# One phase for the second layer's norm, token mix, 28 projection products and key norm, with x and its squares handed over in SBUF

## What is computed

```python
def _rms(x, g):
    y = x * lax.rsqrt(jnp.mean(x * x, axis=-1, keepdims=True) + RMS_EPS)
    return y * g

x  = x + conv_ffn(...)                     # layer 0 ends; its last step is the down projection
h  = _rms(x, norm_mix[1])
xx = 0.5 * (previous token + next token of h) - h      # zero beyond the ends of each group
xr, xw, xk, xv, xa, xg = (h + xx * mu[i] for i in range(6))
r, k, v = xr @ w_r, xk @ w_k, xv @ w_v                 # 1024 x 1024 each
w = tanh(xw @ w1); a = xa @ a1; g = sigmoid(xg @ g1)   # narrow: 128, 128 and 160 columns
kk = k * k_k, divided by its length within each head of 64 channels
```

## Time and profile before

| | us |
|---|---|
| median of 3 runs | 5436.38 |
| lowest and highest of them | 5423.24, 5439.86 |
| the profiled execution, its own time | 5390.18 |
| its span, first to last instruction | 5388.3 |
| its mean granted TensorE clock | 0.887 of full speed |

### The profile page before, as it was taken

How to read it: one execution, slowest core, us unless ns; L and a number is a source line. 1 busy time by engine, 2 the same in 40 slices (tenths; PEclk the granted TensorE clock), 3 DMA queues, 4 the chain that set the end, 5 groups by cost and what they waited for, 6 DMA issues and landing times. The chain is left out here.

```text
span 5388.3 us, 97136 instructions
## 1 busy us (share of the span) xinstructions
PE 4514.7 (84%) x41700; PEld 3690.8 (68%) x41700; DVE 2352.2 (44%) x4075; ACT 1312.4 (24%) x2687; POOL 1311.0 (24%) x915
## 2 busy tenths in 40 slices
PE   2999798999999938876567777777767899999997
PEld 1789667888888827765355555555555588888886
DVE  3011262442425251123577777777773224234341
ACT  1111372111111122222233333333332221111110
POOL 2111133111111101110344444444441131111110
PEclk8999899999999979997587877877788699999998
DMA  3112334113131222211311111111102231221314
GB/s 125 58 59 72 92 97 118 44 48 106 36 117 39 91 69 70 70 59 60 102 41 46 46 41 47 51 39 43 51 31 76 57 105 39 88 65 60 96 35 164
DMA packets 393901, 371.41 MB, mean 69 GB/s; under 512 B 61408, under 2 KB 358752, under 8 KB 392336
## 3 DMA queue, kind: packets, MB, share of 16 engines
q1 hardware_dynamic: 377616, 336.52, 20.4%
q10 hardware_dynamic: 15872, 28.84, 1.4%
HBM read 263.06 MB, written 102.24 MB: 68 GB/s over the span
## 5 line engine op out<-in xcount | busy, mean ns | idle before, releaser
L417 POOL TENSOR_TENSOR f_wlow<-f_raw,f_whigh 128x1024 fp32r<-128x1024 f32 (+1 forms) x152 | 360.2, 2370 | 1678.8 <-ACT f_whigh L477 1678.8
L462 PE MATMUL f_ps<-fx_hh,f_whigh 128*128 128x512 f32 (+1 forms) x2112 | 529.0, 359 | 0.0
L462 PE MATMUL f_ps<-fx_hl,f_whigh 128*128 128x512 f32 (+1 forms) x2112 | 528.0, 359 | 0.0
L462 PE MATMUL f_ps<-fx_hh,f_wlow 128*128 128x512 f32 (+1 forms) x2112 | 527.6, 358 | 0.0
L523 DVE TENSOR_TENSOR f_xo<-f_ps,f_xo 128x512 f32<-128x512 f32 (+1 forms) x192 | 103.7, 596 | 698.9 <-PE f_ps L462 661.0
L477 ACT ACTIVATE f_whigh<-f_raw 128x1024 fp32r<-128x1024 f32 (+1 forms) x152 | 156.7, 1031 | 987.3 <-PE f_ps L462 960.2
L462 PEld LDWEIGHTS f_ps<-fx_hl,f_whigh 128*128 128x128 f32 x2112 | 351.9, 188 | 62.4
L462 PEld LDWEIGHTS f_ps<-fx_hh,f_wlow 128*128 128x128 f32 x2112 | 351.8, 188 | 62.4
L462 PEld LDWEIGHTS f_ps<-fx_hh,f_whigh 128*128 128x128 f32 x2112 | 352.1, 189 | 61.8
L1537 PE MATMUL sc_inv_ps<-sc_tf,sc_bl 64*64 64x64 f32 x6400 | 318.8, 249 | 78.7 <-DVE sc_tf L1878 74.1
L462 PE MATMUL f_ps<-mo_oh,f_whigh 128*128 128x512 f32 (+1 forms) x1440 | 361.3, 359 | 25.4 <-POOL f_wlow L417 25.4
(11 more groups left out here) (318 smaller groups left out, 8720.3 us busy)
## 6 DMA issues: line engine op xcount, KB each, us to landing
f_xo<-xres SPq DMA_DIRECT2D x64, 640.0 KB, 4.0
xres<-f_xo SPq DMA_DIRECT2D x64, 640.0 KB, 2.9
f_raw<-in_ffn_w_gate SPq DMA_DIRECT2D x44, 512.0 KB
f_raw<-in_ffn_w_up SPq DMA_DIRECT2D x44, 512.0 KB
sc_rk<-rkvl SPq DMA_DIRECT2D x80, 256.0 KB, 3.2
f_raw<-in_ffn_w_down SPq DMA_DIRECT2D x32, 448.0 KB
qkv_raw<-in_na_w_qkv SPq DMA_DIRECT2D x24, 512.0 KB, 5.5
qkn<-qkv_qk SPq DMA_DIRECT2D x16, 640.0 KB, 3.6
```

The costliest lines, as they stand in the source:

```text
L417: nc.gpsimd.tensor_tensor(wlow[:, m % 2, 0:kt], raw[:, 0:kt], whigh[:, m % 2, 0:kt].bitcast(F32), ALU.subtract).then_inc(cut_lo, 1)
L462: last = nc.tensor.matmul(ps[:, m % 2, n, 0:count], w[:, m % 2, k], x[:, k, t0:t0 + count], start=(k == 0 and w is whigh and x is xh), sto ...
```

## The change

1. `feed_forward` gets two more outputs. In the last 8 down jobs of layer 0, DVE writes its sum into a kept SBUF tensor `x` and no longer into `xo` (the store to `xres` stays); ACT squares each tile and POOL adds the squares up in `total`.
2. `rms_norm`, `mix_differences`, the six `mixed_product` phases and `unit_keys` go. A new `rwkv_inputs` is one phase. It sums `total` over channels on TensorE, takes root and reciprocal of 128x10 numbers, spreads them to 128x1280 in PSUM, and DVE multiplies `x` by that in place ("normalise"). POOL forms the neighbour sums `near`. The norm's gain and the mix weights are folded into two scales by channel, so a mixed tile is ACT's scaled copy of `x` ("own") plus DVE's `near` times a scale ("blend").
3. The 28 jobs run in the order r, v, w, a, g, k. ACT mixes the tiles of the next kind when its list reaches the last job of the kind before. One buffer `raw` of weights takes the place of two.
4. In the k jobs, ACT squares a finished tile of k, TensorE sums within heads between steps of the next job and spreads the inverted roots, and DVE scales the tile where it lies; SP stores it to `kks`.

```diff
@@ feed_forward, SP, POOL, ACT, DVE
+                    src = x_out[:, i] if x_out is not None and residual[q] >= last_down else xo[:, q % 2]
+                    sp.dma_start(xres[:, i], src).then_inc(stored[q % 2], 16)
...
+                def add_square(i):
+                    pool.wait_ge(last_squared, i + 1)
+                    if i >= 2:
+                        pool.wait_ge(last_totalled, i - 1)
+                    nc.gpsimd.tensor_tensor(total_out[:], total_out[:], square, ALU.add).then_inc(last_totalled, 1)
...
+                    if m >= last_down and x_out is not None:
+                        act.wait_ge(evicted, m + 1)
+                        if i >= 2:
+                            act.wait_ge(last_totalled, i - 1)
+                        nc.scalar.activation(square if i else total_out[:], x_out[:, i], ACT.Square).then_inc(last_squared, 1)
...
+                            old = dst
+                            if m >= last_down and x_out is not None:
+                                dst = x_out[:, i, t0:t0 + count]
+                            last = nc.vector.tensor_tensor(dst, src, old, ALU.add)
@@ new rwkv_inputs: SP
+                sp.dma_start(ones[:], consts["ones"][:, 0:2]).then_inc(small_in, 16)
+                sp.dma_start(ident[:], consts["ident"]).then_inc(small_in, 16)
+                sp.dma_start(block64[:], consts["block64"]).then_inc(small_in, 16)
+                load_weights(0)
...
+                load_weights(1)
+                for m in range(NJ):
+                    if m + 2 < NJ:
+                        load_weights(m + 2)
+                    store(m)
+                    if m >= K0 + 1:
+                        store_key(m - K0 - 1)
@@ POOL
+                low(0)
+                low(1)
+                for k in range(KT):
+                    pool.wait_ge(normed, k + 1)
+                    for a, b in ((1, T_PROMPT - 1), (T_PROMPT + 1, T - 1)):
+                        nc.gpsimd.tensor_tensor(near[:, k, a:b], x[:, k, a - 1:b - 1], x[:, k, a + 1:b + 1], ALU.add)
+                    nc.gpsimd.tensor_copy(near[:, k, 0:T_PROMPT + 1:T_PROMPT], x[:, k, 1:T_PROMPT + 2:T_PROMPT])
+                    nc.gpsimd.tensor_copy(near[:, k, T_PROMPT - 1:T:T_SAMPLE], x[:, k, T_PROMPT - 2:T - 1:T_SAMPLE]).then_inc(near_done, 1)
+                for m in range(2, NJ):
...
+                    low(m)
@@ TensorE
+                for m, (n, i) in enumerate(jobs):
+                    pe.wait_ge(cut_lo, m + 1)
...
+                    for k in range(KT):
+                        if i == 0:
+                            pe.wait_ge(mix_lo, order.index(n) * KT + k + 1)
...
+                        if m >= K0 + 1:
+                            if k == 2:
+                                key_sums(m - K0 - 1)
+                            if k in (4, 5, 6):
+                                key_roots(m - K0 - 1, k - 4)
@@ ACT
+                def own(j):
+                    c, k = divmod(j, KT)
+                    if j >= 3:
+                        act.wait_ge(mix_lo, j - 2)
...
+                    nc.scalar.activation(slot(j), x[:, k], ACT.Copy, scale=own_scale[:, r, k:k + 1]).then_inc(own_done, 1)
...
+                def mix(c):
+                    own(c * KT)
+                    own(c * KT + 1)
+                    for k in range(KT):
+                        if k + 2 < KT:
+                            own(c * KT + k + 2)
+                        high(c * KT + k)
...
+                mix(0)
+                for m, (n, i) in enumerate(jobs):
+                    if m == last_of[n] and n != "k":
+                        mix(order.index(n) + 1)
+                    leave(m)
+                    if m + 2 < NJ:
+                        cut(m + 2)
+                    if n == "k":
+                        key_root(i)
@@ DVE
+                def normalise(k):
+                    nc.vector.tensor_tensor(x[:, k, 0:1024], flat(1), x[:, k, 0:1024], ALU.mult)
+                    nc.vector.tensor_tensor(x[:, k, 1024:T], ps[:, 1, 2, 0:256], x[:, k, 1024:T], ALU.mult).then_inc(normed, 1)
...
+                def mix(c):
+                    for k in range(KT):
+                        blend(c * KT + k)
+                        if k:
+                            low(c * KT + k - 1)
+                        if c == 0 and k + 2 < KT:
+                            normalise(k + 2)
+                    low(c * KT + KT - 1)
```

More of the change, by code:

```diff
@@ L1048, in mixed_product, with rwkv_inputs @@
-def mixed_product(nc, name, h, xx, mu, sources, func, out, out_tile, xh, xl):
-    n, load_tile, zero_first = sources
-    with Phase(nc, name) as ph:
-        raw = ph.sb("raw", [P, 2, KT, P])
-        wh = ph.sb("wh", [P, 2, KT, P], F32R)
-        wl = ph.sb("wl", [P, 2, KT, P], F32R)
+def rwkv_inputs(nc, x, total, gain, mu, w_r, w_k, w_v, w1, a1, g1, k_k, rkvl, kks, consts):
+    rest = g1.shape[1] - P
+    order = "rvwagk"
+    views = {n: w.rearrange("(k p) n -> p k n", p=P) for n, w in zip("rwkvag", (w_r, w1, w_k, w_v, a1, g1))}
+    mu_row = {n: i for i, n in enumerate("rwkvag")}
+    tiles = {"r": KT, "v": KT, "w": 1, "a": 1, "g": 2, "k": KT}
+    out_tile = {"r": 0, "k": KT, "v": 2 * KT, "w": 3 * KT, "a": 3 * KT + 1, "g": 3 * KT + 2}
+    func = {"r": ACT.Copy, "k": ACT.Copy, "v": ACT.Copy, "w": ACT.Tanh, "a": ACT.Copy, "g": ACT.Sigmoid}
+    jobs = [(n, i) for n in order for i in range(tiles[n])]
+    NJ = len(jobs)
+    last_of = {n: max(m for m, job in enumerate(jobs) if job[0] == n) for n in order}
+    K0 = jobs.index(("k", 0))
+    width = lambda m: rest if jobs[m] == ("g", 1) else P
+    halves = (slice(0, HD), slice(HD, P))
+    with Phase(nc, "ri") as ph:
+        xh = ph.sb("xh", [P, KT, T], F32R)
+        xl = ph.sb("xl", [P, KT, T], F32R)
+        near = ph.sb("near", [P, KT, T])
@@ L1063, in mixed_product @@
+        flat = lambda b: ps[:, b, 0:2].rearrange("p g n -> p (g n)")
+        slot = lambda j: total[:] if j % 3 == 2 else mixed[:, j % 3]
         with nc.Block() as block:
@@ L1065, in _, with load_weights @@
             def _(sp):
[L1066 to L1077 removed]
+                def load_weights(m):
+                    n, i = jobs[m]
+                    if m:
+                        sp.wait_ge(cut_lo, m)
+                    if jobs[m] == ("g", 1):
+                        sp.wait_ge(cleared, 1)
+                    sp.dma_start(raw[:, :, 0:width(m)], views[n][:, :, i * P:i * P + width(m)]).then_inc(w_in, 16)
@@ new lines, in _ @@
+                dve.wait_ge(summed, 1)
+                nc.vector.tensor_scalar(rc[:], sums[:, 0:NB], 1.0 / D, RMS_EPS, ALU.mult, ALU.add).then_inc(averaged, 1)
+                dve.wait_ge(rooted, 1)
+                nc.vector.reciprocal(rc[:], rc[:]).then_inc(inverted, 1)
+                dve.wait_ge(gain_in, 128)
+                for n in range(6):
+                    last = nc.vector.tensor_tensor(mus[:, n], mus[:, n], g[:], ALU.mult)
+                last.then_inc(mu_gain, 1)
+                dve.wait_ge(mu_gain, 1)
@@ new lines, in blend, with low @@
+                def blend(j):
+                    c, k = divmod(j, KT)
+                    r = mu_row[order[c]]
+                    dve.wait_ge(own_done, j + 1)
+                    if c == 0:
+                        dve.wait_ge(near_done, k + 1)
+                    nc.vector.scalar_tensor_tensor(slot(j), near[:, k], near_scale[:, r, k:k + 1], slot(j), ALU.mult, ALU.add).then_inc(mix_done, 1)
+                def low(j):
+                    k = j % KT
+                    dve.wait_ge(mix_hi, j + 1)
+                    nc.vector.tensor_tensor(xl[:, k], slot(j), xh[:, k].bitcast(F32), ALU.subtract).then_inc(mix_lo, 1)
@@ L1293 @@
+                dve.wait_ge(spread, 1)
+                normalise(0)
+                normalise(1)
+                for c in range(len(order)):
+                    mix(c)
+                for p in range(KT):
+                    scale_key(p)
 C = 64
```

416 lines of the change are left out of this document (182 added, 234 removed).

## The result

Four executions of the changed kernel have a median of 5288.44 us (5283.62 to 5293.9), four of the kernel before on the same series 5429.81 (5415.59 to 5439.86): ratio 0.9742, 95% interval 0.9715 to 0.9768, that is 141 us less. The forecast was 5325 with a range down to 5290: right in sign, 37 us too high, and the time lies just under the range.

What follows compares the result with a forecast made beforehand. Between layer 0's last products and the scan, TensorE's jobs need 394.2 of 709.3 us; norm, boundaries, slow first jobs and key norm fill the rest. Steps sum to 2480, plus 3 clock: 2483 for 2594.6; 5436.38 less 111.5 gives 5325, range 5290 to 5370.

Steps and rivals of the forecast that it cites:

- first mix and r0: Mixing the first kind's eight tiles and job r0, 1911.5 to 1968: 56.5 us.
- tail: Key norm of the last k tile, bare after k7: leave, square, sums, roots and scaling, store, barrier; 16.5 us.
- clock, set apart: TensorE restarting at half rate after pauses, up to 3.4 us at each of five places; 3 us taken in all.
- 6.3 a tile, 8 tiles 50.4, and 4 at the ends: First mix: POOL's 3.3 added to DVE's blend and low, not normalise, because the two engines block each other.
- The step of 4.05: Mix beside a running job: own waits for low(k-1) to free its slot, then high, then low; 4.05 us.
- norm, differences and r0: Part of the forecast gain, from the old norm and differences phases and job r0: 37 us.
- the 13 us by which the shown runs scatter: Range term for scatter of the old kernel's three shown runs: 13 us, giving 5290 to 5370.
- Better overlap at 5303: Rival: no blocking beyond the one pair, key operations without clock loss; gain 133, 5303 us, chance 0.12.
- The worse first mix: Rival: POOL's four operations a tile each wait for DVE, clock falls in every mix; gain 75, 5361, chance 0.12.
- ACT serialising everything: Rival: ACT's list makes each of 48 mixed tiles take 6.3 us instead of 4.05; 5436, no change, chance 0.03.
- the clock in whole jobs: Rival: TensorE at 1.2 GHz in whole jobs, 11.6 us more each; 5569 with all 21 unpaced jobs, chance 0.02.
- Everything behind it shifted alike: Expected sign: the scan's first DMA 111 us earlier and all that follows moved by the same amount.

Runs made afterwards that it cites:

- near_on_dve: Changed kernel with the neighbour sums of the first mix on DVE instead of POOL: stage 590.9 us, 6.0 more.
- high_first: Changed kernel with ACT's order in a mix turned round, high(k) ahead of own(k+2): stage 557.1 us, 27.8 less; time 5286.72 us, ratio 0.9739.
- the second series: Kernel before and changed kernel measured once more, both unedited, on one chip: 5409.62 and 5304.07 us, ratio 0.9797, 106 us apart.
- the gate held: Kernel before and changed kernel, each with two extra 128x256 products a unit in the layer-1 gate: 5376.03 and 5255.17 us.
- again_after: Changed kernel once more, unedited: 5304.07 us, ratio 0.9797, stage 583.6, gate 205.7.
- three_edits_block_gate: Changed kernel with high ahead of own, late second cut, block products in key norm and in gate: 5209.96 us, ratio 0.9607.

## Why the prediction was wrong, and where it was right

**The stage.** The forecast took 111.5 us off it, 3 of them lost to the clock; the first two profiles differ by 121.5, the means of three by 123.1. Against its steps:

| step | forecast | measured |
|---|---|---|
| phase start | 1892.1 | 1892.6 |
| to POOL's first sum | 19.4 | 18.4 |
| first mix and r0 | 56.5 | 50.5 |
| r1 to r6 | 84.5 | 84.5 |
| r7 to the start of v1 | 37.7 | 36.9 |
| v1 to v6 | 84.5 | 84.7 |
| v7 to the start of g1 | 104.6 | 102.3 |
| g1 to k1 | 40.7 | 39.8 |
| k1 to k7 | 143.5 | 144.4 |
| tail | 16.5 | 19.5 |
| clock, set apart | 3 | in the above |
| scan's first DMA | 2483 | 2473.5 |

The step that was mis-sized most is "6.3 a tile, 8 tiles 50.4, and 4 at the ends": the whole stretch took 50.5 for 56.5, eight steps of 6.02 and 2.3 more, where I had put 6.1 for the ends and the last step of the job; 6 of the 9.5 us are there. That POOL and DVE exclude each other was right: in the rows the times add (2.46, 3.71, 4.94 and 3.08), and with POOL out of the way DVE's durations are nominal (near_on_dve). The Trainium skill (SBUF — State Buffer, "Who interferes with whom") calls it an exclusive lock, held for a whole instruction; both traces agree. But that 6.3 came so near to 6.02 is in part luck. I had added all of POOL's 3.3 to blend and low, and nothing for the normalising or for DVE's wait for `high`. In the rows the step is blend 1.5, that wait 1.2, low 1.9 and normalising 1.6, less some overlap. POOL's larger addition fills the wait and then holds up the low part by only 0.4, and its smaller addition and the copies lie beside the normalising. The step of 4.05 was measured at 4.08, and its chain, own waiting for a slot behind low, was the real one: high_first takes it away and gains 27.8. TensorE's pause was 4.3 ahead of a and 6.4 ahead of g0 (forecast 5 to 7), key jobs 20.6 apart on the mean (20.5), though in two lengths, 19.5 and 21.0, by the clock, down jobs 12.32 apart (12.3), the clock 1.00 in r1 to r6. The tail is 3.0 longer: its spreads ran at half rate (1.98 and 1.97 us for four blocks, 1.09 inside a job), so roots and scaling took 8.3 instead of 5.5. Measured singly, the key norm inside the jobs is worth 29.5 (forecast 33), the hand-over in SBUF 25.6 of the 37 given to norm, differences and r0.

**The time.** The larger part of the miss is the sentence "The three runs shown have a median of 5436.38, 46 above the profiled execution. I subtract the same 111.5", together with "the 13 us by which the shown runs scatter". Three executions don't tell what the kernel before takes: 50 of them have a median of 5417.65 and run from 5384.5 to 5446.2, so the 5436.38 was high and the profiled 5390.18 low. Of the 37 us, 10 are the stage, 7 the fall of the median before from 5436.38 to 5429.81 by one execution more, and the remaining 20 must be what four executions of each kernel happened to draw elsewhere; the second series drew the other way (106). That this lies in the gate and the scan is seen in the profiled executions only, one of each series. The others have a time and a mean clock, and these point the same way: of 58 executions of the kernel before, the eight fastest have 0.880 to 0.888 and the eight slowest 0.870 to 0.877. All 62 have a median of 5417.17, the ten of the changed kernel 5291.2, and this difference, 126, is near the stage's 123. As differences, the intervals of the two series are 126 to 155 and 91 to 128 us. With the gate held the two kernels differ by 120.9. The 46 us between profile and median was to be read in the forecast as a warning: the gate's clock of 0.69 as a mean of 1.00 and 0.50 stood in the same trace. Its range had a term for the scatter of the old kernel's three runs, none for what either kernel does behind the stage. So the term that failed is the starting value with its 13 us of scatter: single executions of the kernel before lie up to 62 us apart, while its stage repeats within 1 us.

**The rivals.** Better overlap at 5303 is nearest to the time, but not by its mechanism: the engines do block each other, and only two of seven key jobs were free of the clock's loss. The worse first mix, ACT serialising everything and the clock in whole jobs didn't come. "Everything behind it shifted alike" was wrong for a single pair of traces: the feed-forward of layer 1 starts 98.4 us earlier in the first pair (4179.7 against 4278.1), not 121.

## What to carry to other kernels

Before forecasting a time, cut the trace at block boundaries and ask which block could run at either clock level. A change's worth is read from its own stage (here within 2.5 us from one trace each), while the whole time needs many executions: with the gate free, two series gave 141 and 106 for a change of 121 to 123.

In a chain over two engines look at the list order of the one that idles: one swap gave 28 us. And many tiny products between long ones cost TensorE their own time (5.4 us a job here) and brought its clock down in most jobs (1.1 more on the mean); one product with a block matrix for each token group cost a third, 2.1, at full clock, and moved the work to DVE, which had room for it in this stage.

## What the hardware showed that was not expected

- TensorE can be busy without a pause at its 1.2 GHz level for over 140 us: 24.00 of 24 us at 0.50, in six successive stretches of again_after. The Trainium skill (TensorE: Matmul & The Clock Gate, "What's actually happening") says that the clock is throttled by default and that activity releases the throttle; if a busy engine is an active one, the level would rise here, and the trace doesn't agree. Two more products of 256 columns a unit brought the block's mean clock from 0.51 to 0.70 up to 0.83 to 0.90. What in the load decides isn't shown. That it is the many small products of the gate was only argued: three_edits_block_gate does without them and still had 0.73, but with TensorE busy only 113 of 156 us.
- Extra work made the kernel faster: the fillers are wasted products, and the kernel before gains 53 us on its chip (5429.41 to 5376.03), more than the 36 forecast. Its gate is 21 and 36 us shorter than in the two traces without fillers (146.7 against 167.9 and 182.7); where the rest lies isn't shown.
- TensorE's clock fell right after the tiny sums in five of seven key jobs, although the engine never paused there (21.02 of 21.02 us busy at 0.92).
- DVE's reciprocal takes 6.5 to 6.8 ns a column (3.35 us for 512, 1.75 for 256), against 0.75 us for the scaled product of two operands of 512 columns.
